# Feed-forward norm of a decoder layer on one core: sums by token, root on 128x4 values, and eight modulation steps and their loads moved

## The reference

```python
mod = c_act @ w_mod[l] + b_mod[l]
sh_a, sc_a, g_a, sh_f, sc_f, g_f = jnp.split(mod, 6, axis=-1)
...                                   # mixer: projection, three head groups
mix = jnp.concatenate([pool_out, gla_out, nsa_out], axis=-1) @ w_out[l]
x = x + g_a[:, None, :] * mix
hf = rms_norm(x, norm_ffn_gain[l]) * (1.0 + sc_f[:, None, :]) + sh_f[:, None, :]
gate_h, up_h = jnp.split(hf @ w_ffn_in[l], 2, axis=-1)
x = x + g_f[:, None, :] * ((jax.nn.silu(gate_h) * up_h) @ w_ffn_out[l])
# rms_norm(x, g) = x * rsqrt(mean(x * x, over features) + 1e-6) * g
```

## Time and profile before

| | before |
|---|---|
| median of three runs | 2580.43 us |
| lowest and highest | 2573.21 and 2581.84 us |
| the profiled execution | 2575.92 us, span 2574.1 us, mean granted TensorE clock 0.977 |
| TensorE busy | 2484.3 us (97%) |
| VectorE, ScalarE, GpSimd busy | 892.7, 805.5, 1225.3 us |
| chain that ended last | TensorE 69%, issue 17%, GpSimd 9%, VectorE 4% |
| moved | 316.03 MB, mean 123 GB/s |

### The profile page before, as it was taken

The page is one execution under the profiler, slowest core; times in us unless marked ns, Lnnn a source line. Parts: engine busy times, 40 slices in busy tenths (PEclk is TensorE's granted clock), DMA queues, the critical chain, the costliest instruction groups (busy, mean ns, idle before and its releaser), DMA issues.

```text
span 2574.1 us, 33226 instructions
## 1 busy us (share of the span) xinstructions
PE 2484.3 (97%) x11685; PEld 2030.8 (79%) x11685; DVE 892.7 (35%) x1370; ACT 805.5 (31%) x1528; POOL 1225.3 (48%) x958
## 2 busy tenths in 40 slices
PE   5989999999899999799999999999999999999999
PEld 3777777887799888678888888888888888888887
DVE  3755333158688677851101110202020102020112
ACT  4324223232566522233222222222222222222221
POOL 3653333445777544434444444444444444444443
PEclk8889999999899999999999999999999999999999
DMA  7753223375212377733333333232333333323233
GB/s 273 238 203 102 66 66 101 107 245 180 95 58 62 132 253 257 262 108 97 92 97 96 92 97 95 93 98 90 98 91 96 97 91 98 94 94 98 90 98 115
DMA packets 86227, 316.03 MB, mean 123 GB/s; under 512 B 9584, under 2 KB 10240, under 8 KB 84736
## 3 DMA queue, kind: packets, MB, share of 16 engines
q1 hardware_dynamic: 84240, 303.31, 36.6%
q10 hardware_dynamic: 1904, 11.62, 1.2%
HBM read 310.69 MB, written 4.19 MB: 122 GB/s over the span
## 4 chain that ended last, share of the span: by engine, by line
PE 69%; issue 17%; POOL 9%; DVE 4%; DMA 0%; ACT 0%; POOLq 0%; SPq 0%; DVEq 0%; ACTq 0%
PE ps L485 60%; POOL wlo L376 8%; PE ps L863 2%; PE ps L852 1%; PE ps L819 1%; DVE pacc L1345 1%; PE ps L560 1%; PE ps L820 1%; PE ps L592 1%; DVE macc L1320 1%; DMA modw<-in_mstream 0%; PE ps L571 0%; DVE xT L1377 0%; PE ps L843 0%; PE ps L833 0%
## 5 line engine op out<-in xcount | busy, mean ns | idle before, releaser
L376 POOL TENSOR_TENSOR wlo<-raw,whi 128x512 fp32r<-128x512 f32 x696 | 927.4, 1334 | 1158.0 <-ACT whi L990 908.9
L990 ACT ACTIVATE whi<-raw 128x512 fp32r<-128x512 f32 x620 | 390.6, 632 | 1304.6 <-PE ps L485 1169.0
L485 PE MATMUL ps<-hfH,whi 128*128 128x512 f32 x1408 | 557.4, 396 | 17.9 <-DVE hfL L1771 13.0
L485 PE MATMUL ps<-hfH,wlo 128*128 128x512 f32 x1408 | 553.2, 393 | 0.0
L485 PE MATMUL ps<-hfL,whi 128*128 128x512 f32 x1408 | 548.0, 389 | 0.0
L485 PEld LDWEIGHTS ps<-hfH,whi 128*128 128x128 f32 x1408 | 265.5, 189 | 72.6 <-issue 13.8
L485 PEld LDWEIGHTS ps<-hfH,wlo 128*128 128x128 f32 x1408 | 265.1, 188 | 61.9
L485 PEld LDWEIGHTS ps<-hfL,whi 128*128 128x128 f32 x1408 | 265.3, 188 | 58.7
L1798 DVE SCALAR_TENSOR_TENSOR x1T<-ps,modc,x1T 128x512 f32<-128x512 f32 x176 | 132.2, 751 | 454.3 <-PE ps L485 454.3
L485 PE MATMUL ps<-huH,whi 128*128 128x512 f32 x704 | 279.2, 397 | 0.5 <-DVE huL L1782 0.5
L485 PE MATMUL ps<-huH,wlo 128*128 128x512 f32 x704 | 279.1, 396 | 0.0
(11 more groups left out here) (281 smaller groups left out, 3065.2 us busy)
## 6 DMA issues: line engine op xcount, KB each, us to landing
raw<-in_wstream SPq DMA_DIRECT2D x370, 512.0 KB, 3.6
modw<-in_mstream SPq DMA_DIRECT2D x160, 512.0 KB, 4.5
modx<-in_mstream SPq DMA_DIRECT2D x32, 512.0 KB, 6.6
xT<-in_xt SPq DMA_DIRECT2D x4, 1024.0 KB, 8.7
w1s<-in_w ACTq DMA_DIRECT2D x2, 2048.0 KB, 9.0
x1T<-in_xt ACTq DMA_DIRECT2D x4, 1024.0 KB, 8.0
out_y<-x1T SPq DMA_DIRECT2D x16, 256.0 KB, 2.0
cmpb<-in_cmp_tab ACTq DMA_DIRECT2D x1, 1024.0 KB, 5.1
```

What stands on the lines that cost most here:

```text
L376: nc.gpsimd.tensor_tensor(wlo[:, s, :], raw[:, r, :], whi[:, s, :].bitcast(F32), ALU.subtract).then_inc(unit_ready, 1)
L485: ins = nc.tensor.matmul(acc, lhs, rhs, start=first and n == 0, stop=last and n == 2)
L990: A(whi[:, k % SPLIT, :], raw[:, k % 8, :], ACT.Copy).then_inc(unit_hi, 1)
```

## The change

`norm_sum` swaps its operands. The squares become the stationary operand, block of 128 tokens by block, and one column of ones moves: `ps[:, 7, t]` holds the sum of token 128 t + p in partition p, 128x4 values in all. Scale and add, reciprocal and root are made on these 128x4 (in `ss`). VectorE then makes four diagonal matrices `diag` from the identity, and TensorE multiplies all ones by each, which puts the root of every token into all partitions of bank 7 again, where `hf_value` reads it. `keep_warm` adds four matmuls whose result nobody reads. In the `hf` loop the low part k goes ahead of hf_value(k + 2). The eight steps of q = 22, d = 4 to 7 go behind the last `hfL`, the loads of m = 184 to 191 from j = 108 to 111 to j = 114 to 117, and the sums of the last two columns to n = 13 and n = 22.

```diff
--- before.py
+++ after.py
@@ -195,7 +195,7 @@
         huH = at("huH", [P, 4, S], F32R, pbase + 4 * KD * S)
         huL = at("huL", [P, 4, S], F32R, pbase + 4 * (KD * S + 4 * S))
         x1sq = at("x1sq", [P, 2, S], F32, tab_base)
-        fvar = at("fvar", [P, S], F32, tab_base + 4 * 2 * S)
+        diag = at("diag", [P, T, P], F32, tab_base + 4 * 2 * S)
         gsil = at("gsil", [P, 2, S], F32, tab_base + 4 * 3 * S)
         hfull = at("hfull", [P, 2, S], F32, tab_base + 4 * 5 * S)
 
@@ -236,6 +236,7 @@
         m_psum, m_hi, m_lo, mixed = sem("m_psum"), sem("m_hi"), sem("m_lo"), sem("mixed")
         x1_landed, x1_ready, x1_sq, x1_summed, u_ready, f_var, f_std, f_v, f_hi, f_ready = (sem(n) for n in (
             "x1_landed", "x1_ready", "x1_sq", "x1_summed", "u_ready", "f_var", "f_std", "f_v", "f_hi", "f_ready"))
+        f_diag, f_spread = sem("f_diag"), sem("f_spread")
         gate_done, gate_saved, up_saved, h_hi, h_lo, y_done, y_added = (sem(n) for n in (
             "gate_done", "gate_saved", "up_saved", "h_hi", "h_lo", "y_done", "y_added"))
         stored = sem("stored")
@@ -350,9 +351,12 @@
                     load_mod(8 * i + 125 + 2 * s, (2 * s + 1) % 4)
             for j in range(106, 124):
                 load_units(j, j % 4)
-                if j < 112:
+                if j < 108:
                     load_mod(2 * j - 32, (2 * j - 32) % 4)
                     load_mod(2 * j - 31, (2 * j - 31) % 4)
+                if 114 <= j < 118:
+                    load_mod(2 * j - 44, (2 * j - 44) % 4)
+                    load_mod(2 * j - 43, (2 * j - 43) % 4)
             with sp.Fori(0, (UNITS // 2 - 124) // 4) as i:
                 for s in range(4):
                     load_units(4 * i + 124 + s, s)
@@ -914,8 +918,10 @@
             def norm_sum(c):
 
                 pe.wait_ge(x1_sq, c + 1)
-                nc.tensor.matmul(ps[:, 7, :], ones[:, :], x1sq[:, c % 2, :], start=c == 0,
-                                 stop=c == KD - 1).then_inc(x1_summed, 1)
+                for t in range(T):
+                    ins = nc.tensor.matmul(ps[:, 7, t:t + 1], x1sq[:, c % 2, t * P:(t + 1) * P], ones[:, 0:1],
+                                           start=c == 0 and t == 0, stop=c == KD - 1, skip_group_check=True)
+                ins.then_inc(x1_summed, 1)
 
             for c in range(KD):
                 if c >= 4:
@@ -930,8 +936,19 @@
                     sum_pool_columns(6)
                 if c and c % 2 == 0:
                     sum_columns(14 + c // 2, 6)
+            def keep_warm(columns):
+
+                nc.tensor.matmul(ps[:, 4, 0:columns], ones[:, :], x1T[:, 0, 0:columns], start=True, stop=True)
+
+            keep_warm(S // 2)
             norm_sum(KD - 1)
-
+            keep_warm(S)
+            for t in range(T):
+                pe.wait_ge(f_diag, t + 1)
+                ins = nc.tensor.matmul(ps[:, 7, t * P:(t + 1) * P], ones[:, :], diag[:, t, :], start=True, stop=True)
+            ins.then_inc(f_spread, 1)
+            keep_warm(S)
+            keep_warm(S)
 
             def hf_ready(k):
                 return f_ready, k + 1
@@ -941,8 +958,8 @@
                     for b in range(2):
                         n = 6 * kq + 2 * p + b
                         weight_unit(U_FFN + n, n % 4, 2 * p + b, kq, hfH, hfL, KD, hf_ready)
-                        if n in (4, 20):
-                            sum_columns({4: 22, 20: 23}[n], 6)
+                        if n in (13, 22):
+                            sum_columns({13: 22, 22: 23}[n], 6)
             pe.wait_ge(mod_read, 25)
             for b in range(2):
                 for kq in range(4):
@@ -1248,7 +1265,7 @@
             square(KD - 1)
 
             act.wait_ge(f_var, 1)
-            A(ps[:, 7, :], fvar[:, :], ACT.Sqrt).then_inc(f_std, 1)
+            A(ss[:, T:2 * T], ss[:, 0:T], ACT.Sqrt).then_inc(f_std, 1)
 
             def hf_high(k):
                 act.wait_ge(f_v, k + 1)
@@ -1742,7 +1759,7 @@
                                        in1=x1T[:, c, :], op0=ALU.mult, op1=ALU.add).then_inc(x1_ready, 1)
                 if c == 1:
                     finish_pool_mod(6)
-                for n in range(4 * c, 4 * c + 4):
+                for n in range(4 * c, 4 * c + (4 if c < KD - 1 else 0)):
                     if n % 8 == 0 and n:
                         finish_mod(14 + n // 8, 6)
                     if n == 8:
@@ -1752,25 +1769,28 @@
                     mod_step(15 + n // 8, n % 8, 1)
 
             dve.wait_ge(x1_summed, KD)
-            own(V.tensor_scalar(fvar[:, :], ps[:, 7, :], 1.0 / D, EPS, ALU.mult, ALU.add))
-            V.reciprocal(fvar[:, :], fvar[:, :]).then_inc(f_var, 1)
+            own(V.tensor_scalar(ss[:, 0:T], ps[:, 7, 0:T], 1.0 / D, EPS, ALU.mult, ALU.add))
+            V.reciprocal(ss[:, 0:T], ss[:, 0:T]).then_inc(f_var, 1)
+            dve.wait_ge(f_std, 1)
+            for t in range(T):
+                V.tensor_scalar(diag[:, t, :], ident[:, :], ss[:, T + t:T + t + 1], None, ALU.mult).then_inc(f_diag, 1)
 
             def hf_value(k):
                 V.scalar_tensor_tensor(out=uT[:, k, :], in0=x1T[:, k, :], scalar=acol[:, k:k + 1], in1=ps[:, 7, :],
                                        op0=ALU.mult, op1=ALU.mult).then_inc(f_v, 1)
 
             dve.wait_ge(u_ready, 1)
-            dve.wait_ge(f_std, 1)
+            dve.wait_ge(f_spread, 1)
             hf_value(0)
             hf_value(1)
             for k in range(KD):
-                if k + 2 < KD:
-                    hf_value(k + 2)
                 dve.wait_ge(f_v, k + 1)
                 dve.wait_ge(f_hi, k + 1)
                 V.scalar_tensor_tensor(out=hfL[:, k, :], in0=uT[:, k, :], scalar=modc[:, M_SHF + k:M_SHF + k + 1],
                                        in1=hfH[:, k, :].bitcast(F32), op0=ALU.add,
                                        op1=ALU.subtract).then_inc(f_ready, 1)
+                if k + 2 < KD:
+                    hf_value(k + 2)
 
             def hidden(n, b, bank):
                 dve.wait_ge(gate_saved, n + 1)
@@ -1782,6 +1802,9 @@
                 V.tensor_tensor(huL[:, b, :], hfull[:, b % 2, :], huH[:, b, :].bitcast(F32),
                                 ALU.subtract).then_inc(h_lo, 1)
 
+            for d in range(4, 8):
+                mod_step(22, d, 0)
+                mod_step(22, d, 1)
             finish_mod(22, 6)
             add_mod(23)
             finish_mod(23, 6)
```

## The result

| | before | changed |
|---|---|---|
| median | 2580.43 us (7 runs, 2573.21 to 2585.1) | 2565.99 us (7 runs, 2561.4 to 2568.42) |
| ratio | | 0.9942, 95% interval 0.9931 to 0.9952 |
| the profiled execution | 2575.92 us | 2567.31 us |

The change makes the kernel faster by 0.58%, which is 15.0 us of the median before (12.4 to 17.8); the two medians differ by 14.4. A second set on another occasion gave 0.9936 (0.9922 to 0.9949).

What follows compares the result with a forecast made beforehand. TensorE bounds the kernel. 7.7 us (first unit earlier) + 6.6 (second pause) - 0.6 (sums) = 13.7 us off: 2562.2 from the profiled run, 2566.7 from the median; forecast 2565 us, range 2557 to 2573.

Steps and rivals of the forecast that it cites:

- rival 2: The keep_warm fillers hold TensorE's full clock throughout: 14.7 us off, 2564 us; chance 0.18.
- rival 4: ScalarE isn't free at once behind its table load, root starts 1.0 us later: 12.7 us off, 2566; chance 0.04.
- The queue of 5.3 us: Ahead of the variance, eight macc steps on VectorE delay it; 5.3 us of TensorE's 13.0 us wait.
- The second pause, 6.6 us: TensorE's 4.9 us wait for wlo at n=10, plus slow restart; moving loads on SP's queue wins 6.6 us.
- Scale and add, reciprocal, root, diagonals, spreading: Between last sum and hf_value(0): shorter 128x4 steps plus two new ones, hf_value(0) moving from 1092.38 to 1084.5.
- The table load: ScalarE's 1.28 us load for the root, right behind the last square; over before 1082.4, so it stays hidden.
- The order of the `hf` loop: hfL(0) no longer stands behind hf_value(2) on VectorE; wins 0.4 to 0.5 us.
- The sums by token, +0.6 us: First fifteen chunks in TensorE's stream: eight one-column records replace two wide matmuls, 0.04 us more each, +0.6 us.
- The clock: TensorE's clock expected to fall once, at the squares or the first unit; priced at 1.0 us.
- ScalarE behind n=22: h_high(0) and the n=25 split follow the moved sums; ready after 3.9 us, needed at 5.4, hidden.
- The eight moved steps: Modulation steps behind the last hfL cost VectorE some 8 us, hidden where it later waits 28.14 us.
- Rival 3: Second pause moves to another unit through a late load or split; only 7.1 us left, 2572; chance 0.10.

Runs made afterwards that it cites:

- e1: Kernel before with the moved loads, the eight moved steps and the sums at n=13 and n=22, norm as before: 2570.48 us, ratio 0.9965.
- e3: Kernel before with only the loads of m=184 to 191 moved to j=114 to 117: 2573.91 us, ratio 0.997.
- e6: Changed kernel with the old order of the hf loop, hf_value(k + 2) ahead of the low part k: 2567.56 us, ratio 0.9938.
- e7: Changed kernel with the one-column sums of the first fifteen chunks made twice: 2588.34 us, ratio 1.0024.
- e5: The changed kernel run again, unaltered: 2565.01 us, ratio 0.9936.
- e8: Changed kernel with the first four units taken together, k by k: 2567.41 us, ratio 0.9938.
- e9: Changed kernel with the first two units taken together, k by k: 2564.61 us, ratio 0.9934.
- e4: Changed kernel without its four keep_warm matmuls: 2566.73 us, ratio 0.9948.
- e10: Changed kernel with only the two keep_warm matmuls ahead of the spreading: 2568.64 us, ratio 0.995.
- e11: Changed kernel with only the two keep_warm matmuls behind the spreading: 2565.76 us, ratio 0.9941.
- e2: Changed kernel with steps, loads and the two sums put back, leaving norm by tokens, fillers and hf order: 2581.36 us, ratio 1.0.

## Why the prediction was right

The forecast was 2565 us; the median is 2565.99. Point by point:

- **The profiled execution and the median.** The sum of 13.7 gave 2562.2 from the profiled run and 2566.7 from the median. The second was the right base: the profile of before had run 6 us ahead of the others before the stage. 2565 lay between the two, for no reason that a run bears out. That half a step towards the wrong base did no harm is luck: the clock gave back 0.8 us that the sum had not counted. From the median, 15.1 less 0.6 for the earlier sums gives 2565.9. The seven runs spread over 7 us, so their times can't tell the forecast from rival 2 (2564) or rival 4 (2566); the trace does.
- **The queue of 5.3 us** is gone in e1 (wait 13.0 to 7.7) and in the changed kernel. Right to 0.1 us against the kernel before; in e3 the same queue is 6.1 us.
- **The second pause, 6.6 us.** 6.2 us in e3 by the table, 6.6 for the pause itself, from SP's order alone. Right: the last of the loads j=108 to 111 is issued at 1088.18, ahead of the end of the last sum. So was the cover: `load_units(115)` is issued at 1124.37, n=18 starts some 19 us later, at 1143.1.
- **Scale and add, reciprocal, root, diagonals, spreading.** Worked out as 2.3 us from the last sum to `hf_value(0)`; measured 2.3, twice. The first unit ends 7.2 us behind that (7.05 worked out).
- **The table load.** It ends at 1088.96 and the root runs from 1089.21, when the reciprocal is done. By the drain of some 1380 ns that the Trainium skill ("ScalarE: Activation LUTs", What ACT_TABLE_LOAD costs) gives, read as the prediction did, behind the load, it could not have started before 1090.3. This trace disagrees, and there is no such drain ahead of the load either (the last square ends at 1087.66, the load starts at 1087.68); rival 4 is excluded.
- **The order of the `hf` loop.** 0.4 to 0.5 predicted, 0.37 measured (e6).
- **The sums by token, +0.6 us.** 0.5 to 0.6 measured. The price of 0.9 us for eight short records holds (e7).
- **The clock.** This is the term that was off: it counted a fall that did not come in the changed kernel. I took one fall, at 1.0 us, as the likely case (rival 2, the fillers hold it, at 0.18). With all four fillers it held in five profiles of six (changed, e5, e6, e7, e8) and fell in one (e9), so what rival 2 describes is what happened in the changed kernel, and 0.18 for it was too low. The size was near: 0.8 us from 14.3 predicted behind the last sum to 15.1 measured, 1.3 us at the first product of e9. The place was not: the late start costs it all, and a first unit at half clock can cost nothing (e4). The fillers' own worth is 0.9 to 1.2 us (e4), and in one profile each neither pair alone gives it (e10, e11). The prediction also misread its window of the earlier trace rows. Of the 26 matmuls there, 20 have one column and six are products of 512 columns; the row of short ones is 24 long, from 891.13 us, and the clock fell behind six products more. The changed kernel has the same 24 from 897.96 us, and half clock from 900.55.
- **ScalarE behind n=22.** Predicted ready 3.9 us behind the sums with 1.5 us of cover. The lines of ScalarE and GpSimd in the changed kernel, behind sums that end at 1160.5:

```profile
1161.73 0.63 ACT L1284 ACTIVATE huH<-hfull 128x512 fp32r<-128x512 f32 x1 [6.27 <-DVE hfull L1797]
1162.27 1.14 ACT L1007 ACTIVATE whi<-raw 128x512 fp32r<-128x512 f32 x2
...
1162.96 5.58 POOL L380 TENSOR_TENSOR wlo<-raw,whi 128x512 fp32r<-128x512 f32 x4 [6.61 <-ACT whi L1007]
```

The first of the four low parts is done at about 1164.4, 3.9 us behind; no wait of TensorE.

- **The eight moved steps.** They took 11.0 us and not 8, but VectorE still waited 6.0 and 6.5 us for the two sums (28.14 before the second one). Hidden, as said.
- **What the prediction did not have.** It added the parts up as if each had its own price. The sum came out right because all of them were there: alone, the norm is worth nothing that the runs can measure (e2), although at full clock each of its steps takes the time worked out for it.

Rival 3 (the pause moves) is excluded by the waits after. Why the clock fell in e9 and not in e8, which has the same instructions up to the first product, stays open; the runs differ by chance there.

## What to carry to other kernels

Before shortening a chain of small steps, look at what stands in the queue in front of it and at what ends the next wait behind it: here the shorter arithmetic was worth nothing until the queue on VectorE was moved, and 1.0 us of it went into a pause that a load's place in SP's order had fixed. Measure a part of a change together with the rest as well as alone. Choose the point from which two traces are compared with care: here it moved some parts by 0.6 to 0.9 us. A filler matmul belongs where its length at half clock still fits, not directly in front of the matmul on the path. And if the consumer is fed more slowly than it works, let it take two tiles per piece of input, but no more than the weight buffers can give back in time.

## What the hardware showed that I had not expected

- Short matmuls did not hold the clock even when TensorE was never idle: in e7, behind 2.7 us of 24 one-column records without a pause, products start every 0.43 us in place of 0.23, at five of seven places. The Trainium skill ("TensorE: Matmul & The Clock Gate", HAM oscillation) tells of waits as the cause; here it happened without one.
- The same instructions can meet the clock up or down: with all fillers the spreading took 1.16 us in five profiles and 1.76 in one.
- One stretch of e2 ran 2% slow at a granted clock of 1.00: 0.2333 us from one matmul start to the next for 28 us, where the same units start 0.229 apart in the kernel before. No run here says why.
